# In the even mixer ScalarE rounds the weights, and the sample convolution becomes a product of shifted views

## The reference

```python
def even_mixer(h, hist_pool, hist_conv, start_pos, w_in, pool_w, pool_scale, conv_w, conv_b, ln_g, ln_b, w_out):
    z = jnp.einsum('btd,de->bte', h, w_in)
    a_in, a_gate, b_val, b_glu, b_gate = jnp.split(z, ...)          # five parts of 1024 channels
    a = multiscale_pool_minus_self(a_full, start_pos)               # windows 2, 4, 8, 16
    a = jnp.einsum('btgc,gce->btge', a, pool_w).reshape(Bn, T, W_A) * pool_scale
    a = a * jax.nn.silu(a_gate)
    v = b_val * jax.nn.sigmoid(b_glu)
    v_full = jnp.concatenate([hist_conv, v], axis=1)                # 30 rows of history
    c = causal_dwconv(v_full, conv_w) + conv_b                      # 31 taps per channel
    c = jax.nn.silu(layernorm(c, ln_g, ln_b)) * jax.nn.silu(b_gate)
    y = jnp.einsum('bte,ed->btd', jnp.concatenate([a, c], axis=-1), w_out)
```

## Time and profile before

| | |
|---|---|
| median of 3 runs | 2838.85 us (2838.82 to 2842.92) |
| profiled execution | 2840.13 us, of it the span 2838.4 us |
| granted TensorE clock, mean | 0.939 |
| TensorE busy | 88% of the span |
| VectorE busy | 50% |
| GpSimd busy | 45% |
| ScalarE busy | 15% |

### The profile page before, as it was taken

The page is one execution under the profiler, slowest core; times in us unless marked ns, Lnnn a source line. Parts: engine busy times, 40 slices in busy tenths (PEclk is TensorE's granted clock), DMA queues, the critical chain, the costliest instruction groups (busy, mean ns, idle before and its releaser), DMA issues. The chain is left out here.

```text
span 2838.4 us, 37980 instructions
## 1 busy us (share of the span) xinstructions
PE 2506.3 (88%) x14950; PEld 2403.9 (85%) x14950; DVE 1411.8 (50%) x1582; ACT 430.7 (15%) x728; POOL 1289.9 (45%) x842
## 2 busy tenths in 40 slices
PE   4967879777699689999799999999999997799996
PEld 4967879777699669888799999999999996698886
DVE  5999999999744452332622232322312234523324
ACT  3110110101111321122310000000000003211212
POOL 2734444434355454344544444444444445543452
PEclk7988999888899789999899999999999997999998
DMA  2111111111121132233011111111111111322331
GB/s 91 54 37 44 48 47 51 46 29 45 53 73 57 38 112 78 67 115 111 26 46 46 45 45 41 45 45 41 45 45 45 41 44 37 112 79 67 114 111 63
DMA packets 224013, 168.55 MB, mean 59 GB/s; under 512 B 10746, under 2 KB 219138, under 8 KB 223922
## 3 DMA queue, kind: packets, MB, share of 16 engines
q1 hardware_dynamic: 214002, 156.78, 18.0%
q10 hardware_dynamic: 9920, 10.48, 1.1%
HBM read 152.29 MB, written 14.93 MB: 59 GB/s over the span
## 5 line engine op out<-in xcount | busy, mean ns | idle before, releaser
L147 POOL TENSOR_TENSOR w_hi<-w_raw,ones 128x512 fp32r<-128x512 f32 x404 | 576.3, 1427 | 1407.4 <-PE PS L211 1225.5
L211 PE MATMUL PS<-h_hi,w_hi 128*128 128x364 f32 x2880 | 646.8, 333 | 61.0 <-DVE e_V L828 39.1
L150 POOL TENSOR_TENSOR w_lo<-w_raw,w_hi 128x512 fp32r<-128x512 f32 x404 | 644.1, 1594 | 31.7
L211 PE MATMUL PS<-h_hi,w_lo 128*128 128x364 f32 x2880 | 642.4, 332 | 0.0
L211 PE MATMUL PS<-h_lo,w_hi 128*128 128x364 f32 x2880 | 641.6, 331 | 0.0
L211 PEld LDWEIGHTS PS<-h_hi,w_hi 128*128 128x128 f32 x2880 | 502.8, 190 | 66.7 <-DVE e_V L828 40.3
L211 PEld LDWEIGHTS PS<-h_hi,w_lo 128*128 128x128 f32 x2880 | 506.6, 190 | 0.0
L211 PEld LDWEIGHTS PS<-h_lo,w_hi 128*128 128x128 f32 x2880 | 505.7, 190 | 0.0
L851 DVE SCALAR_TENSOR_TENSOR e_C<-e_V,prm,e_C 128x1024 f32<-128x1024 f32 x240 | 322.8, 1345 | 0.3
L211 PE MATMUL PS<-y_hi,w_hi 128*128 128x364 f32 x1152 | 261.6, 336 | 61.7 <-ACT e_GS L702 25.9
L211 PEld LDWEIGHTS PS<-y_hi,w_hi 128*128 128x128 f32 x1152 | 201.5, 192 | 69.5 <-issue 45.0
(11 more groups left out here) (194 smaller groups left out, 2164.0 us busy)
## 6 DMA issues: line engine op xcount, KB each, us to landing
w_raw<-in_w_in_odd SPq DMA_DIRECT2D x128, 256.0 KB, 2.8
w_raw<-in_w_in_even SPq DMA_DIRECT2D x80, 256.0 KB, 2.9
a_KV<-in_cache_mem_k SPq DMA_DIRECT2D x64, 256.0 KB, 4.9
a_KV<-in_cache_mem_v SPq DMA_DIRECT2D x64, 256.0 KB, 4.3
w_raw<-in_w_out_even SPq DMA_DIRECT2D x32, 256.0 KB, 2.7
w_raw<-in_w_k SPq DMA_DIRECT2D x32, 256.0 KB, 2.9
w_raw<-in_w_v SPq DMA_DIRECT2D x32, 256.0 KB, 2.8
w_raw<-in_w_q SPq DMA_DIRECT2D x32, 256.0 KB, 2.8
```

The source lines that it names most:

```text
L147: c.nc.gpsimd.tensor_tensor(by_128(c.Wh[:, s, :]), by_128(c.Wraw[:, s % RAW, :]), ones, ALU.mult).then_inc(self.w_hi, 1)
L150: c.nc.gpsimd.tensor_tensor(c.Wl[:, s, :], c.Wraw[:, s % RAW, :], c.Wh[:, s, :].bitcast(F32), ALU.subtract).then_inc(self.w_split, 1)
L211: mm = pe.matmul(ps[:, q, 0:PART], w, a[:, q * PART:(q + 1) * PART], start=first and n == 0, stop=last and n == 2)
```

## The change

In the even mixer alone, `split_all` on GpSimd is replaced by `low_all`: GpSimd makes only the remainders `w_lo`, and ScalarE makes the rounded halves `w_hi` with a copy (`high`). ScalarE's order is by hand, so `highs_behind(tile)` is put behind the points at which a tile's result has been waited for. It makes all units up to the one that takes the slot of the tile's last unit. The other mixer and both attentions keep `split_all`. The sample rows' taps leave the loop: `conv_samples(j)` behind `pooled_low(j)` multiplies for four samples at a time all 31 shifted views of `e_VS` with the 31 taps (128x992 elements), sums over the innermost axis (128x32 results), and adds the bias at the end: five instructions for a chunk in the place of 31. The sample attention's column tiles stand in both kernels alike.

```diff
+    def high(self, act, u):
+        c = self.c
+        act.wait_ge(self.raw_in[u % RAW], 16 * (u // RAW + 1))
+        if u >= SPLIT:
+            act.wait_ge(self.half, 2 * (u - SPLIT) + 2)
+        c.nc.scalar.activation(c.Wh[:, u % SPLIT, :], c.Wraw[:, u % RAW, :], ACT.Copy).then_inc(self.w_hi, 1)
+
+    def low_all(self, pool, units):
+        c = self.c
+        for u in range(units):
+            pool.wait_ge(self.w_hi, u + 1)
+            c.nc.gpsimd.tensor_tensor(c.Wl[:, u % SPLIT, :], c.Wraw[:, u % RAW, :], c.Wh[:, u % SPLIT, :].bitcast(F32),
+                                      ALU.subtract).then_inc(self.w_split, 1)
...
+        if before_sum is not None:
+            before_sum()
         act.wait_ge(self.sum, 1)
...
-    TAPS = 2 * CONV
+    SIDE, SIDE_OPS = 10, 5
+    TAPS = CONV + SIDE_OPS
+    HALF = NB // 2
...
-            G.split_all(pool, 116)
+            G.low_all(pool, UNITS)
...
+            def highs_behind(tile):
+                for u in range(made[0], min(last_unit[tile] + SPLIT + 1, UNITS)):
+                    G.high(act, u)
+                    made[0] = u + 1
+
             def evacuate(tile, out, func, **more):
                 wait_result(act, tile)
                 s.activation(parts(out), bank(tile), func, **more).then_inc(freed(tile), 1)
+                highs_behind(tile)
...
-            norm.scalar(act)
+            norm.scalar_std(act, first_highs)
+            for u in range(RAW, SPLIT):
+                G.high(act, u)
+                made[0] = u + 1
+            norm.scalar_split(act)
             for j in range(KD):
                 if j % 2 == 0 and j:
+                    highs_behind(("pool", j - 1))
                     ya_high(j - 2)
                     ya_high(j - 1)
+                if j % 2 and j > 1:
+                    for k in range(1, KD, 2):
+                        highs_behind(("outa", j // 2 - 1, k))
...
                 conv_tail(j)
+                highs_behind(("val", j))
...
+            highs_behind(("outa", 3, 3))
             swish(0)
             swish(1)
             for g in range(4):
+                for k in range(1, KD, 2):
+                    highs_behind(("outb", g - 1, k) if g else ("outa", 3, k))
                 yb_high(2 * g)
                 yb_high(2 * g + 1)
...
+            def conv_samples(j):
+                done = TAPS * j + SIDE
+                taps = c.prm[:, j, ROW_CONV_W:ROW_CONV_W + CONV].unsqueeze(1).unsqueeze(1).to_broadcast([P, HALF, TS, CONV])
+                products = PT[:, 0:HALF * TS * CONV].rearrange("p (b t n) -> p b t n", b=HALF, t=TS)
+                side = CB[:, j % 2, T:TA]
+                dve.wait_ge(m_lo, j + 1)
+                for h in range(2):
+                    base = VS[:, HALF * h:HALF * (h + 1), 0:TS]
+                    windows = bass.AP(base.tensor, base.offset, [list(d) for d in base.ap] + [[1, CONV]])
+                    if h:
+                        dve.wait_ge(cv, done + 2)
+                    v.tensor_tensor(products, windows, taps, ALU.mult).then_inc(cv, 1)
+                    dve.wait_ge(cv, done + 2 * h + 1)
+                    v.tensor_reduce(side[:, HALF * TS * h:HALF * TS * (h + 1)].rearrange("p (b t) -> p b t", b=HALF),
+                                    products, AX_X, ALU.add).then_inc(cv, 1)
+                dve.wait_ge(cv, done + 4)
+                v.tensor_scalar(side, side, c.prm[:, j, ROW_CONV_B:ROW_CONV_B + 1], None, ALU.add).then_inc(cv, 1)
...
                     pooled_low(j)
-                    dve.wait_ge(m_lo, j + 1)
+                    conv_samples(j)
```

More of the change, by code:

```diff
@@ L252, in __init__, with scalar_std @@
         self.DG = self.SQ[:, :, :].rearrange("p a n -> p (a n)")[:, 0:self.TILES * P]
-    def scalar_std(self, act):
+    def scalar_std(self, act, before_sum=None):
         c = self.c
@@ L540, in block_even @@
     order, number, end = even_plan()
+    last_unit, u = {}, 0
+    for tile in order:
+        u += {"outa": tile[-1] % 2 == 0, "outb": tile[-1] % 2 == 0, "pool": tile[1] % 2 == 0, "sum": 0}.get(tile[0], 2)
+        last_unit[tile] = u - 1
+    UNITS = u
     w_in, w_out = r["w_in_even"][0], r["w_out_even"][0]
@@ L698, in _ @@
             s = nc.scalar
+            made = [0]
+            def highs_behind(tile):
+                for u in range(made[0], min(last_unit[tile] + SPLIT + 1, UNITS)):
+                    G.high(act, u)
+                    made[0] = u + 1
             def evacuate(tile, out, func, **more):
@@ L702, in evacuate, with first_highs @@
                 s.activation(parts(out), bank(tile), func, **more).then_inc(freed(tile), 1)
+                highs_behind(tile)
+            def first_highs():
+                for u in range(RAW):
+                    G.high(act, u)
+                    made[0] = u + 1
             def store_conv(j):
@@ L773, in _ @@
                 evacuate(("agate", j), GS[:, j % 2, :], ACT.Silu)
+            highs_behind(("pool", KD - 1))
             ya_high(KD - 2)
@@ L840, in conv @@
                         dve.wait_ge(stats, 3 * (j - 1))
-                outs = (CB[:, j % 2, 0:T], CB[:, j % 2, T:TA].rearrange("p (b t) -> p b t", b=NB))
                 for n in range(first, last):
-                    ins = (V[:, n:n + T], VS[:, :, n:n + TS])
                     tap = c.prm[:, j, ROW_CONV_W + n:ROW_CONV_W + n + 1]
[L845 to L851, removed]
+                    if n == 0:
+                        v.tensor_scalar(CB[:, j % 2, 0:T], V[:, 0:T], tap, c.prm[:, j, ROW_CONV_B:ROW_CONV_B + 1],
+                                        ALU.mult, ALU.add).then_inc(cv, 1)
+                    else:
+                        dve.wait_ge(cv, TAPS * j + n + (SIDE_OPS if n >= SIDE else 0))
+                        v.scalar_tensor_tensor(CB[:, j % 2, 0:T], V[:, n:n + T], tap, CB[:, j % 2, 0:T],
+                                               ALU.mult, ALU.add).then_inc(cv, 1)
```

## The result

The median fell from 2840.13 us to 2758.43 us (four runs of each); the ratio on record is 0.9707, with a 95% interval of 0.9692 to 0.9721. The forecast was 2774, and the time lies in the range. The span of the profiled execution went from 2838.4 to 2758.9 us, 79.5 less.

What follows compares the result with a forecast made beforehand. VectorE was taken to set the pace in the even mixer's eight chunks (653 us). The terms -77 - 20 + 41 - 10 + 2 + 3 - 4 = -65 us gave a median of 2774 us, range 2748 to 2806.

Steps and rivals of the forecast that it cites:

- GpSimd's rounding goes, -77: Even mixer's chunks: 81 of 163 GpSimd instructions leave, each costing VectorE 0.95 us; -77 us, bounds -83 to -53.
- The tap chain, -20: VectorE's tap loop: prompt taps follow directly after 1.31 us against 1.39 for the pair; -19, and -1 for first taps.
- rival 4: VectorE's tap chain has no wait: next prompt tap starts 1.20 us after the last, 27 us less, 2747; chance 0.09.
- The product, +41: VectorE's multiplications, sums and bias for the sample rows: 5.2 us a chunk, +41 us for eight.
- Waits filled, -10: VectorE's waits of 7.0 us (adds) and 3.7 us (`ya`) are covered by the product's 5 us: about -10.
- TensorE level, +3: Before the next `value`, TensorE's path comes level with VectorE's: 1 us for each of three groups, +3.
- rival 2: TensorE and its weights become a second bound in the chunks: +20 + 9 us, 2803; chance 0.18.
- ScalarE's copies, 0: ScalarE's 116 copies of 0.60 us: late agate units, `e_Mh` and squares come at cost 0.
- The first pooling, +2: First ain tile's units wait for the sigmoid of glu 0, some 3 us; VectorE's first pooling loses about 2.
- the start, -4: First sums of squares: six adds take 7.9 us instead of 13.2 without GpSimd's splits; with remainders elsewhere (up to +2), -4.
- Rival 3: A lone GpSimd instruction blocks VectorE for its full 1.30 us (2803), or the product's views run at half rate (2791); chance 0.10.
- Rival 6: Slower: ScalarE's copy and GpSimd's remainder stand in front of every tile, 1.9 us a pair, +110 us, 2884; chance 0.05.

Runs made afterwards that it cites:

- the two kernels with zeros: GpSimd writes zeros for the remainders, reading nothing: against the whole change (product) 2712.25 us, against ScalarE's rounding alone (sample taps kept) 2691.37 us.

## Why the prediction was right

*The bound.* VectorE was read as the bound of the chunks, TensorE with 110 us of pauses to give. Right: with 36 us less of VectorE's busy time the chunks are 32 us shorter, and with 62 us more they are 59 longer.

*GpSimd's rounding goes, -77.* The mechanism was right, and the price of a GpSimd instruction in the kernel before too: 0.95 taken, 154.5 / 163 = 0.95 measured. With the sample taps kept, the term comes out as it stands: 154.5 - 76.4 = 78 us. In the whole change it is 154.5 - 56.3 = 98 us, since beside the bare chain of prompt taps and the product a remainder costs 0.67. The step treated the price as a property of GpSimd's instruction; it depends on what VectorE runs beside it. That is 21 us, more than the whole error of the forecast.

*The tap chain, -20.* A dependent tap was taken to start after 1.31 us, and it does after 1.32; in the same trace an output add, which does not depend on the tap ahead of it, starts 1.19 us after it (241.81 - 240.62 in the third chunk's rows above). So rival 4 falls. The Trainium skill ("VectorE: DVE Perf Modes", The DRAIN you can't avoid) says that a semaphore after each instruction costs nothing extra; this kernel's chain does not agree, though no run leaves the wait out of it.

*The product, +41.* Taken at 1.18 and 1.16 us, measured at 1.19 and 1.19; overlapping views and the broadcast cost nothing that can be seen. From start to start, the two kernels with zeros give 41 us for it and 25 less for the chain with its first taps: together +16 instead of +21. The chain saves more than was taken: over all taps a lone one comes to 1.30 us and a pair to 1.40, where 1.31 and 1.39 were taken.

*Waits filled, -10, and TensorE level, +3.* The adds' and `ya`'s waits fell from 10.7 to 2.5 us, as forecast. But the same 5 us pushed TensorE back, and where +3 was taken there are 6.6 us of `value` behind the first (15.7 - 9.1), and 8 us more for the squares, which the forecast had put at 0. VectorE's waits in the chunks are 19.8 us instead of 13.4, so together the term is +6 instead of -7. This is rival 2 in small, by 13 us, and it is what the place of the product settles: behind the adds the squares' wait falls to 1.6 us, and the two halves in two places take the adds' wait away as well.

*ScalarE's copies, 0.* Right where it was tried: agate's units, forecast to be late at no cost, gain nothing when made earlier. A copy takes 0.62 us, the taken 0.60.

*The first pooling, +2, and the start, -4.* VectorE's first pooling lost 0.6 us, which is among the waits above; the six sums take 8.3 us instead of 13.2, and the first `value`, which waits for TensorE, is 2.3 us earlier.

The measured terms in the chunks are -98 + 16 + 6 = -76 us, and 75.8 were measured. The forecast had -61 there, 15 short: the first term was 21 too small, the chain and product 5 too dear, the waits 11 too favourable (+6 against -7 and the first pooling's +2). The mechanism was right; that the number lies as near as it does is in part luck, since these errors partly cancel. The prediction named two signs by which it would fail, a price of the lone remainder that is not near 0.95 and a queue of ScalarE's that delays what VectorE reads. Both came in part: 0.67 on average, and 9.2 us of waiting for the squares.

Rival 3, dear remainders or views, was wrong in its direction: a hit costs 0.91 to 1.01 us and not 1.30, and the views cost nothing. Rival 6 did not come: TensorE waits 9.7 us for remainders in all, a part of it by the ambiguity shown above.

## What to carry to other kernels

When another engine's instructions hold up those of the bound engine, price it by a kernel in which the other only writes, over exactly the same stretch, and compare the bound engine's busy time: it gave 0.95, 0.91, 0.78 and 0.67 us an instruction, by what ran beside it. Compare busy time, short gaps and waits apart: here they close to the measured time, and the run time alone would have misled. Two edits that attack the same loss must be measured one by one: here ScalarE's rounding alone gave the whole gain, and on top of it the product gained nothing until it was moved.

A group's mean tells who was held up, not who caused it. The sample tap's 745 ns looked like a dear small instruction, but it costs only 0.07 to 0.10 us undisturbed (1.39 or 1.40 for a pair, 1.32 or 1.30 for a lone tap); with the small taps gone and GpSimd's count as before, the prompt taps took most of the blocks over (1345 to 1646 ns).

## What the runs showed of the hardware

A 64-element VectorE instruction with two SBUF inputs takes 0.276 us, and on average 745 ns beside 163 GpSimd instructions that read SBUF, 463 ns beside 84, and 276 beside 84 that only write. With GpSimd only writing, a prompt tap's mean is 1283 ns against 1432. The Trainium skill ("SBUF — State Buffer", Who interferes with whom) says that a VectorE instruction with two SBUF inputs contends with a GpSimd instruction that reads SBUF, and not with one that only writes it; these runs agree. A VectorE instruction that is hit lasts 0.91 us longer on average in the whole change and 1.01 with tap pairs, most of the 1.30 that GpSimd's takes undisturbed. Sums with one SBUF input were not lengthened by it (1186 ns with and without). A multiplication whose input is 31 overlapping views, broadcast against 31 taps, runs at the rate of a plain one: 1.19 us for 992 elements, where the plain one takes 1.23 for 1038.
